# Half of the modulation loads moved from ahead of the first projection unit to beside units 0 and 1

## The chip, the cores and the metric

The kernel runs on one core of one Trainium2 chip. The metric is the device time of one execution in microseconds, lower is better. The parts of the core that matter here: TensorE (matrix products, PE in the profile, its weight loads PEld), VectorE (DVE), ScalarE (ACT), GpSimd (POOL), SyncE (SP), which issues all transfers from one queue, and the DMA engines.

## What is computed

A backbone of two layers on 512 latent tokens and 256 context tokens of width 1024. Only the beginning of layer 0 is touched:

```python
def rms_norm(x, g):
    xf = x.astype(jnp.float32)
    y = xf * lax.rsqrt(jnp.mean(xf * xf, axis=-1, keepdims=True) + EPS)
    return (y * g.astype(jnp.float32)).astype(x.dtype)

def modulate(x, g, shift, scale):
    return rms_norm(x, g) * (1 + scale) + shift
...
        mod_lat = jnp.split((silu_c @ w_mod[l] + b_mod[l])[:, None, :], N_MOD, axis=-1)
        mod_ctx = jnp.split((silu_cc @ w_mod[l] + b_mod[l])[None, None, :], N_MOD, axis=-1)
        a_lat = modulate(x, norm1_g[l], mod_lat[0], mod_lat[1])
        a_ctx = modulate(h, norm1_g[l], mod_ctx[0], mod_ctx[1])
...
    aq, ak, av, rq, rk, rv, rgf, rgb, fu = split_proj(a_lat @ w_in)
    cq, ck, cv, crq, crk, crv, crgf, crgb, cfu = split_proj(a_ctx @ w_in)
```

So the input projection needs the normalized tokens, and these need a shift (`mod[0]`) and a scale (`mod[1]`), each 1024 wide for two conditioning vectors, from 8 MB of `w_mod`.

## The kernel before

Everything is held transposed: X is [128, 8 tiles of features, 768 tokens]. Every fp32 operand of a large product is split into a high and a low part (`Whi`/`Wlo`, `Ahi`/`Alo`), and three products of the parts are added. ScalarE makes the high part of weights (`hi_static`), GpSimd the low one (`low_part`, `low_parts`: Wlo = raw - Whi); the semaphores are `hi_done` and `lo_done`.

The program is written by hand, one stream for each engine, and every stream runs in its written order. The input projection of layer 0 has 18 units. Units 0 to 3 make the first 512 columns: unit u multiplies the feature tiles 2u and 2u+1 into six banks (psA, psB, psS), 36 products of 512 columns. Unit 0 is `first_unit`, and unit 3, the last of its group, is `whole`: it goes bank by bank, and needs the low weights at its first product (`lo_done` 4).

**The modulation loads.** 16 loads of 512 KB (`modst`, six slots) bring the shift and scale rows of `w_mod`. Here they are m0 to m15, in the order of their issue. The even ones are for VectorE (`start(i)` takes m2i): each is multiplied with `csil` and added to an accumulator, four operations, so that after four loads a chunk of the scale (chunk 2, then chunk 3) is there as partial sums over partitions. The odd ones are for TensorE (`first_mod(i)` in TensorE's stream takes m(2i+1)): two products with a two-column stationary `csil` and 512 moving columns, four records in the trace, here called row products; four loads give a row of a shift chunk (chunk 0, then chunk 1). Chunk 0 and 2 serve the feature tiles 0 to 3, chunk 1 and 3 the tiles 4 to 7. A load into a slot waits for the one that used it last: m14 for `start(4)`, m15 for `first_mod(4)`.

VectorE's accumulator is summed over partitions by `mod_sums` (eight transposes on TensorE) and `mod_reduce` (two reductions and an addition on VectorE). TensorE's row is copied from PSUM by ScalarE (`row_copy`), turned by TensorE (`turn_row`) and gets its bias on VectorE (`shifts`).

**The norm.** X comes in as Xin (12 loads of 256 KB), is turned by TensorE (`x_turn(m)`, m = 0..7) and copied by ScalarE (`x_copy`); ScalarE squares it with sums. ScalarE's `norm_root` and VectorE's reciprocal give rstd, which `spread(0)` writes to ps6 (latent) and ps7 (context), one row on all partitions. Then for each tile j: VectorE `norm_full(0, j)` multiplies X by the gain and by ps6 or ps7 (two operations, `a_full`), ScalarE `norm_hi` adds the shift and rounds (`a_hi`; for odd j it writes a second, full copy too, and signals behind it), and the low part of A is VectorE's (`norm_low`, even j) or GpSimd's (`norm`, odd j, semaphore `a_lo_odd`).

In this program all 16 loads come first, and TensorE's stream has all row products, turns and sums ahead of `first_unit`, with filler products (`keep_clock_early`) between them. Behind the modulation loads SP issues the weights of units 0 and 1, then small loads (rope, sinks, tables), then the weights of unit 2.

Notation: `a_hi` n means that n tiles have signalled; "A 5" is the low part of A's tile 5; "W 2" is the low part of unit 2's weights.

## Time and profile before

| | us |
|---|---|
| time, median of 3 runs | 1581.91 (1579.78 to 1582.76) |
| the profiled execution | 1579.42 |
| its span on the core | 1577.5 |
| TensorE busy | 1551.3 (98%) |
| VectorE busy | 921.4 (58%) |
| ScalarE busy | 592.6 (38%) |
| GpSimd busy | 639.5 (41%) |

The span runs from the first to the last instruction of the core; 1.9 us of the execution lie around it. The page cuts the span into 40 slices of 39 us. TensorE is busy at nine tenths or more in all of them but the first, where it has six, so the start is the only stretch where it waits for long. DMA is at nine tenths in the first slice, and at two to four in most others. TensorE's granted clock is 0.999 of full speed over the span. "Busy" counts pipelined products whose times overlap; a step of work is therefore read as the distance between two starts.

### The profile page before, as it was taken

How to read it: one execution, taken by the hardware profiler on the slowest of the kernel's cores; microseconds unless marked ns; L12 is line 12 of the kernel's file. 1: busy time of each engine (PE TensorE's matmuls, PEld its weight loads, DVE VectorE, ACT ScalarE, POOL GpSimd, SP SyncE). 2: the span in 40 equal slices, each digit the busy share in tenths (PEclk: the TensorE clock that was granted, in tenths of full speed). 3: DMA queues.
4: the chain of work that ended last, by engine and by line, in shares of the span. 5: the costliest groups of instructions: out<-in, count | busy, mean ns of one | idle time of the engine just before them, and what ended most of it. 6: DMA issues, size and time to landing. Idle time of an engine off the chain costs nothing.

```text
span 1577.5 us, 22772 instructions
## 1 busy us (share of the span) xinstructions
PE 1551.3 (98%) x8718; PEld 1333.8 (85%) x8718; DVE 921.4 (58%) x1464; ACT 592.6 (38%) x982; POOL 639.5 (41%) x350
## 2 busy tenths in 40 slices
PE   6999999999999999999999999999999999999999
PEld 2888898989888888888888998888997888888887
DVE  5977988766765746545463668687645432233232
ACT  4632267743432121222212244435753422333332
POOL 0535478942333323233232464336004444444443
PEclk9999999999999999999999999999999999999999
DMA  9343203033243434344443433230102333333332
GB/s 329 126 142 105 68 18 108 27 108 107 74 131 120 134 107 134 108 133 133 115 126 107 145 111 106 68 92 29 41 4 83 89 94 95 101 97 93 94 105 95
DMA packets 169473, 161.73 MB, mean 103 GB/s; under 512 B 6548, under 2 KB 133928, under 8 KB 169384
## 3 DMA queue, kind: packets, MB, share of 16 engines
q1 hardware_dynamic: 169384, 160.48, 33.4%
q8 instruction: 63, 1.03, 0.3%
q14 instruction: 26, 0.21, 0.0%
HBM read 158.37 MB, written 2.10 MB: 102 GB/s over the span
## 4 chain that ended last, share of the span: by engine, by line
PE 92%; DVE 2%; DMA 1%; issue 1%; ACT 1%; POOL 1%; SPq 0%; POOLq 0%; ACTq 0%
PE psB L2195 31%; PE psA L2195 31%; PE psA L1930 6%; PE psB L1930 6%; PE ps L2165 4%; PE psS L1930 4%; PE psS L1743 2%; PE ps L1743 1%; DMA modst<-in_w_mod_dram 1%; PE psS L2086 1%; PE psA L2140 1%; PE psB L2140 1%; PE psS L1763 1%; PE psB L2141 1%; PE psA L2141 1%
## 5 line engine op out<-in xcount | busy, mean ns | idle before, releaser
L592 POOL TENSOR_TENSOR Wlo<-raw,Whi 128x1024 fp32r<-128x1024 f32 x156 | 380.7, 2441 | 729.5 <-ACT Whi L759 719.9
L759 ACT ACTIVATE Whi<-raw 128x1024 fp32r<-128x1024 f32 x181 | 191.7, 1059 | 677.2 <-PE psB L2195 346.4
L1347 DVE SCALAR_TENSOR_TENSOR X<-psB,modT,X 128x256 f32<-128x256 f32 (+1 forms) x104 | 67.2, 665 | 130.2 <-PE psB L2195 130.0
L1347 DVE SCALAR_TENSOR_TENSOR X<-psA,modT,X 128x256 f32<-128x256 f32 (+1 forms) x104 | 67.0, 663 | 89.6 <-PE psA L2195 89.6
L1177 DVE SCALAR_TENSOR_TENSOR macc<-modraw,csil,macc 128x512 f32<-128x512 f32 x126 | 111.8, 944 | 1.3 <-DMA modraw<-in_w_mod_dram 1.2
L1604 DVE TENSOR_TENSOR Hlo<-Ab,Hhi 128x512 fp32r<-128x512 f32 (+2 forms) x68 | 72.7, 1069 | 54.2 <-ACT Hhi L1050 54.2
L1602 DVE TENSOR_TENSOR Ab<-psA,Tb 128x512 f32<-128x512 f32 (+2 forms) x34 | 26.7, 784 | 129.4 <-ACT Tb L1042 129.4
L2195 PE MATMUL psB<-Ahi,Whi 128*128 128x512 f32 (+1 forms) x424 | 89.5, 357 | 0.0
L2195 PE MATMUL psB<-Ahi,Wlo 128*128 128x512 f32 (+1 forms) x424 | 88.9, 356 | 0.0
L2195 PE MATMUL psB<-Alo,Whi 128*128 128x512 f32 (+1 forms) x424 | 88.9, 356 | 0.0
L2195 PE MATMUL psA<-Ahi,Whi 128*128 128x512 f32 (+1 forms) x416 | 88.8, 358 | 0.0
L2195 PE MATMUL psA<-Alo,Whi 128*128 128x512 f32 (+1 forms) x416 | 87.8, 355 | 0.0
L2195 PE MATMUL psA<-Ahi,Wlo 128*128 128x512 f32 (+1 forms) x416 | 87.8, 355 | 0.0
L2195 PE MATMUL psA<-Hhi,Whi 128*128 128x512 f32 (+1 forms) x368 | 82.9, 358 | 0.0
L2195 PE MATMUL psB<-Hhi,Whi 128*128 128x512 f32 (+1 forms) x368 | 82.8, 358 | 0.1
L2195 PE MATMUL psB<-Hhi,Wlo 128*128 128x512 f32 (+1 forms) x368 | 82.2, 356 | 0.0
L2195 PE MATMUL psB<-Hlo,Whi 128*128 128x512 f32 (+1 forms) x368 | 82.1, 355 | 0.0
L2195 PE MATMUL psA<-Hlo,Whi 128*128 128x512 f32 (+1 forms) x368 | 82.1, 356 | 0.0
L2195 PE MATMUL psA<-Hhi,Wlo 128*128 128x512 f32 (+1 forms) x368 | 82.0, 355 | 0.0
L2165 PE MATMUL ps<-Pk,PTs 128*128 128x64 f32 x640 | 80.7, 270 | 1.2 <-DVE Alo L1536 0.9
L2195 PEld LDWEIGHTS psB<-Ahi,Wlo 128*128 128x128 f32 x424 | 71.6, 189 | 11.6
L2195 PEld LDWEIGHTS psB<-Alo,Whi 128*128 128x128 f32 x424 | 71.6, 189 | 11.6
(383 smaller groups left out, 3332.9 us busy)
## 6 DMA issues: line engine op xcount, KB each, us to landing
raw<-in_w_ff_dram SPq DMA_DIRECT2D x135, 512.0 KB, 4.0
modraw<-in_w_mod_dram SPq DMA_DIRECT2D x72, 512.0 KB, 4.2
raw<-in_w_in_dram SPq DMA_DIRECT2D x36, 512.0 KB, 3.7
modst<-in_w_mod_dram SPq DMA_DIRECT2D x16, 512.0 KB, 7.2
raw<-in_w_out_dram SPq DMA_DIRECT2D x16, 512.0 KB, 3.7
modat<-in_w_mod_dram SPq DMA_DIRECT2D x8, 512.0 KB, 4.6
macc<-in_w_ff_dram SPq DMA_DIRECT2D x5, 512.0 KB, 3.5
Xin<-in_x_dram SPq DMA_DIRECT2D x8, 256.0 KB, 7.9
```

What stands on the lines that cost most here:

```text
L592: nc.gpsimd.tensor_tensor(Wlo[:, s, :], raw[:, s, :], Whi[:, s, :], ALU.subtract).then_inc(S["lo_done"], 1)
L759: nc.scalar.activation(whis[slot], raws[slot], ACT.Copy).then_inc(S["hi_done"], 1)
L1177: ins = V.scalar_tensor_tensor(out=acc[:, s, :], in0=src[:, kk * MCH:(kk + 1) * MCH], scalar=col, in1=acc[:, s, :], op0=ALU.mult, op1=ALU.add)
L1347: last = V.scalar_tensor_tensor(out=X[:, m, c0:c1], in0=pair[p][:, c0:c1], scalar=modT[:, l, 8 * chunk + m, s:s + 1], in1=X[:, m, c0:c1], ...
L1602: V.tensor_tensor(Ab[:, k % 2, c0:c1], pair[k % 2][:, at + c0:at + c1], Tb[:, k % 2, c0:c1], ALU.mult).then_inc(S["h_full"], 1)
L1604: V.tensor_tensor(Hlo[:, hpar, k, c0:c1], Ab[:, k % 2, c0:c1], Hhi[:, hpar, k, c0:c1], ALU.subtract).then_inc(S["h_lo"], 1)
L1743: return nc.tensor.transpose(out, in_, ident[0:n, 0:n])
L1930: return mm(tokbank[t][:, 0:w], (Ahi, Alo)[x][:, k, t * P:(t + 1) * P], (Whi, Wlo)[y][:, uu % 2, cs], start=first, stop=fin)
L2140: mm(out, q, hi_keys, start=True, stop=False)
L2141: last = mm(out, q, lo_keys, start=False, stop=True)
L2165: last = mm((ps6, ps7)[b % 2][:, h * HD:(h + 1) * HD], PTs[:, it % 2, i * P:(i + 1) * P], Pk[:, kt, P + (h // 4) * HD:P + (h // 4 + 1) * H ...
L2195: last = mm(dst[:, c0:c1], weights[w][:, off:off + P], x[:, i, c0:c1], start=(opens and kind == 0 and i == 0), stop=(closes and kind == 2 ...
```

## The change

- Order of loads: x and ctx are issued behind m0 and m1, then m2 to m7, then the weights of units 0 and 1, then m8 to m15.
- TensorE: only the row products of m1, m3, m5, m7 stay ahead of `first_unit`. Those of m9 and m11 stand inside unit 0, those of m13 and m15 behind it. The turn of row 1 stands inside unit 1, and so do the sums of chunk 3, now eight products of the accumulator with a column of ones (`last_sums`) into ps7 in the place of eight transposes and two reductions. Twelve filler products stand ahead of unit 0.
- VectorE: norm_full 0 and 1 and norm_low 0 come first, then start(4) and start(5), norm_full 2 and 3, norm_low 2, start(6) and start(7), the two additions, the gain, and the tiles 4 to 7.
- ps7 is needed for the second row, so ScalarE copies its 256 columns of rstd for context tokens to `rb_context` in SBUF, and VectorE's context half of every norm_full(0, j) reads that.
- ScalarE: row_copy(1) stands behind the conversion of unit 2's weights, and that ahead of norm_hi 4. GpSimd: W 2 stands between A 3 and A 5, and W 3 behind A 7, one by one, where a loop did W 2 and W 3 behind A 7.

```diff
-    for i in range(16):
-            first_mod(i)
             if i == 2:
                 x_load(0, "xa_in")
-            if i == 4:
                 x_load(1, "xb_in")
-        for u in range(2):
-            w_load(u, u, r2(u), proj_src(0, u), True)
+            if i == 8:
+                for u in range(2):
+                    w_load(u, u, r2(u), proj_src(0, u), True)
+            first_mod(i)
...
-                norm(0)
-                low_parts(2, 10)
+                norm(0, 1, 4)
+                low_part(2)
+                norm(0, 5)
+                low_part(3)
+                low_parts(4, 10)
...
+        act.wait_ge(S["rb_ready"], 1)
+        nc.scalar.activation(rb_context, ps7[:, 0:CTX], ACT.Copy).then_inc(S["rb_copied"], 1)
         hi_static(0)
...
-                    if k == 1:
-                        hi_static(1)
+                    if k in (1, 3):
+                        hi_static(1 + k // 2)
+                    if k == 3:
+                        row_copy(1)
...
-        for i in range(6):
+        for i in range(4):
             start(i)
         mod_reduce(0, 2, 0)
-        shifts(0)
-        start(6)
-        norm_root(0)
-        start(7)
+        first_chunk(0, "row_turned", 1, psS[:, 0:8])
         dve.wait_ge(S["mod_evac"], 2)
         gain(0, 0, 0, 4)
+        norm_root(0)
         dve.wait_ge(S["x_ready"], KT)
         norm_full(0, 0)
-        shifts(1)
         norm_full(0, 1)
-        mod_reduce(0, 3, 1, 2, (psS[:, 0:512], psS[:, 512:1024]))
+        start(4)
+        start(5)
+        norm_full(0, 2)
+        norm_full(0, 3)
+        for i in range(6, 8):
+            start(i)
+        first_chunk(1, "row_turned", 2, ps7[:, 0:8])
+        first_chunk(3, "modp_ready", 2, ps7[:, 8:16])
         dve.wait_ge(S["mod_evac"], 4)
         gain(0, 0, 4, 8)
-        for j in range(2, KT):
+        for j in range(4, KT):
             norm_full(0, j)
...
+        def last_sums():
+
+            pe.wait_ge(S["mod_first"], 8)
+            pe.wait_ge(S["mod_step"], 24)
+            pe.wait_ge(S["mod_evac"], 3)
+            for t in range(4):
+                for s in range(2):
+                    at = 8 + 2 * t + s
+                    last = mm(ps7[:, at:at + 1], macc[:, s, t * P:(t + 1) * P], ones[:, :], start=(t == 0 and s == 0), stop=(t == 3 and s == 1))
+            last.then_inc(S["modp_ready"], 1)
...
                 pe.wait_ge(S["lo_done"], 1)
                 for t in ts:
                     products(0, 0, 1, t)
+                pe.wait_ge(S["rb_copied"], 1)
+                first_mod(4)
                 pe.wait_ge(S["a_hi"], 2)
                 for t in ts:
                     products(1, 0, 0, t)
                     products(1, 0, 1, t)
+                first_mod(5)
                 pe.wait_ge(*a_lo(0, 1))
...
                     first_unit()
+                    first_mod(6)
+                    first_mod(7)
                     continue
...
+                if l == 0 and u == 1:
+                    turn_row(1)
...
+                    if l == 0 and u == 1:
+                        last_sums()
```

VectorE, from the first norm_full of layer 0, before (the names are output <- inputs; Tb and Ab hold the tiles of `norm_full`, ps7 the context half of rstd):

```order
L1239 SCALAR_TENSOR_TENSOR Tb<-X,gs,ps7 128x256 [waits rb_ready,x_ready,dve]
L1239 SCALAR_TENSOR_TENSOR Tb<-X,gs,ps6 128x512
L1319 TENSOR_TENSOR modT<-psS,bmodT 128x8 [waits row_turned]
L1239 SCALAR_TENSOR_TENSOR Tb<-X,gs,ps7 128x256
L1239 SCALAR_TENSOR_TENSOR Tb<-X,gs,ps6 128x512
L1227 SCALAR_TENSOR_TENSOR Alo<-Tb,modT,Ahi 128x256 [waits a_hi]
L1227 SCALAR_TENSOR_TENSOR Alo<-Tb,modT,Ahi 128x512
L1204 TENSOR_REDUCE modT<-psS 128x4 [waits modp_ready]
L1204 TENSOR_REDUCE modT<-psS 128x4
L1207 TENSOR_TENSOR modT<-modT,bmodT 128x8 [waits mod_red]
L1213 SCALAR_TENSOR_TENSOR gs<-modT,parT 128x8 [waits mod_evac]
```

and the same place after (sqb is where `rb_context` lies):

```order
L1247 SCALAR_TENSOR_TENSOR Tb<-X,gs,sqb 128x256
L1247 SCALAR_TENSOR_TENSOR Tb<-X,gs,ps6 128x512
L1233 SCALAR_TENSOR_TENSOR Alo<-Tb,modT,Ahi 128x256 [waits a_hi]
L1233 SCALAR_TENSOR_TENSOR Alo<-Tb,modT,Ahi 128x512
L1181 TENSOR_SCALAR macc<-modst,csil 128x512 [waits modst_in2]
L1181 TENSOR_SCALAR macc<-modst,csil 128x512
L1183 SCALAR_TENSOR_TENSOR macc<-modst,csil,macc 128x512 [waits mod_step] x2
L1183 SCALAR_TENSOR_TENSOR macc<-modst,csil,macc 128x512 [waits mod_step,modst_in4]
L1183 SCALAR_TENSOR_TENSOR macc<-modst,csil,macc 128x512 [waits mod_first]
L1183 SCALAR_TENSOR_TENSOR macc<-modst,csil,macc 128x512 [waits mod_step] x2
L1247 SCALAR_TENSOR_TENSOR Ab<-X,gs,sqb 128x256
```

start(4) and start(5), eight operations on macc, now stand between the tiles 1 and 2, where the reductions stood; start(6) and start(7) follow behind tile 3.

TensorE in unit 1 before, behind its first high products:

```order
L1930 MATMUL psS<-Whi,Ahi 128x512 x4
L1930 MATMUL psA<-Whi,Alo 128x512 [waits a_lo_even]
L1930 MATMUL psA<-Whi,Alo 128x512
L1930 MATMUL psB<-Whi,Alo 128x512 x2
L1930 MATMUL psS<-Whi,Alo 128x512 x2
L1930 MATMUL psA<-Whi,Alo 128x512 [waits a_lo_odd]
L1930 MATMUL psA<-Whi,Alo 128x512
L1930 MATMUL psB<-Whi,Alo 128x512 x2
L1930 MATMUL psS<-Whi,Alo 128x512 x2
L1930 MATMUL psA<-Wlo,Ahi 128x512 [waits lo_done]
```

and after:

```order
L1956 MATMUL psS<-Whi,Ahi 128x512 x4
L1755 MATMUL ps<-ident,sqb 128x2 [waits row_copied]
L1755 MATMUL ps<-ident,sqb 128x2 x3
L1956 MATMUL psA<-Whi,Alo 128x512 [waits a_lo_even]
...
L1956 MATMUL psS<-Whi,Alo 128x512 x2
L1868 MATMUL ps<-ones,macc 128x1 [waits mod_evac,mod_step,mod_first]
L1868 MATMUL ps<-ones,macc 128x1 x7
L1956 MATMUL psA<-Wlo,Ahi 128x512 [waits lo_done]
```

The turn of row 1 and the sums of chunk 3 now stand inside the unit, each with a wait of its own: for ScalarE's copy, and for VectorE's start(7) and chunk 1's addition.

## Rows read from the trace of the kernel before

**Rows 1.** The page: span, and busy time of TensorE (share) xinstructions.

```profile
span 1577.5 us, 22772 instructions
...
PE 1551.3 (98%) x8718; PEld 1333.8 (85%) x8718; DVE 921.4 (58%) x1464; ACT 592.6 (38%) x982; POOL 639.5 (41%) x350
```

**Rows 2.** Windows: stretch, length, busy PE, PEld, DVE, ACT, POOL, PEclk, DMA, GB/s.

```profile
20.00:25.00 5.00, 3.29 (x17) 1.55 (x16) 0.95 (x2) 4.05 (x11) 0.00 (x0) 1.00 1.05 388
```

**Rows 3.** Timeline of TensorE: start, duration, engine, line, operation, out<-in, shape xcount [idle].

```profile
15.21 1.52 PE L1743 MATMUL psA<-ident,Xin 128*128 128x128 f32 x6 [2.90 <-DMA Xin<-in_ctx_dram]
...
26.61 1.88 PE L1837 MATMUL psS<-modst,csil 128*2 128x512 f32 x4
...
30.21 1.09 PE L1743 MATMUL ps<-ident,macc 128*128 128x128 f32 x8
31.24 5.31 PE L1837 MATMUL psS<-modst,csil 128*2 128x512 f32 x12
37.20 0.84 PE L1743 MATMUL ps<-ident,rstd 128*128 128x128 f32 x6 [0.66 <-DVE rstd L1220]
...
40.87 0.40 PE L1743 MATMUL psS<-ident,sqb 2*128 2x2 f32 x4
...
44.33 0.47 PE L1891 MATMUL psA<-Whi,Ahi 128*128 128x512 f32 x1
...
52.75 1.22 PE L1930 MATMUL psA<-Whi,Ahi 128*128 128x512 f32 x4
...
69.44 0.39 PE L1930 MATMUL psA<-Whi,Ahi 128*128 128x512 f32 x1
```

**Rows 4.** Timeline of VectorE.

```profile
24.69 2.74 DVE L1177 SCALAR_TENSOR_TENSOR macc<-modst,csil,macc 128x512 f32<-128x512 f32 x4 [4.04 <-DMA modst<-in_w_mod_dram]
...
32.75 1.28 DVE L1204 TENSOR_REDUCE modT<-ps 128x4 f32<-128x512 f32 x2
...
39.79 1.14 DVE L1239 SCALAR_TENSOR_TENSOR Tb<-X,gs,ps 128x256 f32<-128x256 f32 x2
...
42.47 1.15 DVE L1227 SCALAR_TENSOR_TENSOR Alo<-Tb,modT,Ahi 128x256 fp32r<-128x256 f32 x2
...
48.60 2.19 DVE L1239 SCALAR_TENSOR_TENSOR Ab<-X,gs,ps 128x256 f32<-128x256 f32 x4
...
104.18 1.29 DVE L1204 TENSOR_REDUCE modT<-ps 128x4 f32<-128x512 f32 x2 [7.37 <-PE ps L1743]
```

**Rows 5.** Timeline of ScalarE.

```profile
39.89 0.59 ACT L865 ACTIVATE sqb<-psS 2x512 f32<-2x512 f32 x1 [5.33 <-PE psS L1837]
...
44.60 1.04 ACT L759 ACTIVATE Whi<-raw 128x1024 fp32r<-128x1024 f32 x1
49.77 2.17 ACT L809 ACTIVATE Ahi<-Ab,modT 128x256 fp32r<-128x256 f32 x4 [4.12 <-DVE Ab L1239]
51.84 1.11 ACT L809 ACTIVATE Ab<-Ab,modT 128x256 f32<-128x256 f32 x2
```

**Rows 6.** Timeline of GpSimd and VectorE, where both work, single instructions.

```profile
43.79 2.40 POOL L592 TENSOR_TENSOR Wlo<-raw,Whi 128x1024 fp32r<-128x1024 f32 x1 [9.63 <-DVE Alo L1227]
...
48.50 1.85 POOL L620 TENSOR_TENSOR Alo<-Tb,Ahi 128x768 fp32r<-128x768 f32 x1
...
60.36 2.08 DVE L1175 TENSOR_SCALAR macc<-modraw,csil 128x512 f32<-128x512 f32 x1
...
62.36 2.89 DVE L1177 SCALAR_TENSOR_TENSOR macc<-modraw,csil,macc 128x512 f32<-128x512 f32 x1
64.66 2.84 POOL L592 TENSOR_TENSOR Wlo<-raw,Whi 128x1024 fp32r<-128x1024 f32 x1
```

**Rows 7.** Timeline of TensorE: four products of a tile with a column of ones.

```profile
376.48 0.95 PE L1763 MATMUL psS<-ones,Ab 128*128 128x1 f32 x8
```

**Rows 8.** SP's issues of the small loads (timeline), and landing times of modst (tile).

```profile
34.58 0.47 SPq L472 DMA_DIRECT2D rope<-in_table_dram  x1
...
37.95 0.91 SPq L437 DMA_DIRECT2D tmpt<-in_fourier_w_dram  x2
...
DMA to landing us min/median/max: 3.8/7.2/11.5
```

More of the change, by code:

```diff
@@ L613, in rotate, with norm @@
             nc.gpsimd.tensor_tensor(v, tmp[:, 0:256], tmp[:, 256:512], ALU.add).then_inc(out_sem, 1)
-        def norm(n):
+        def norm(n, j0=1, j1=KT):
             c0, c1 = NORMS[n][2]
-            for j in range(1, KT, 2):
+            for j in range(j0, j1, 2):
                 pool.wait_ge(S["a_hi"], 8 * n + j + 1)
@@ L878, in _ @@
         x_square(1, 1)
+        for t in range(2, NT):
+            x_square(t, 1)
         row_copy(0)
+        norm_root(0)
         x_copy(6)
-        x_square(2, 1)
         x_copy(7)
-        for t in (3, 4, 5):
-            x_square(t, 1)
-        norm_root(0)
-        row_copy(1)
+        act.wait_ge(S["rb_ready"], 1)
+        nc.scalar.activation(rb_context, ps7[:, 0:CTX], ACT.Copy).then_inc(S["rb_copied"], 1)
         hi_static(0)
@@ L1836, in first_mod @@
             for kk in range(2):
-                last = mm(psS[0:2, 512 * c:512 * c + 512], csil[:, 2 * part + kk, :], modst[:, slot, kk * MCH:(kk + 1) * MCH],
+                last = mm((psS, ps7)[c][0:2, 0:512], csil[:, 2 * part + kk, :], modst[:, slot, kk * MCH:(kk + 1) * MCH],
                           start=(part == 0 and kk == 0), stop=(part == 3 and kk == 1))
```

59 lines of the change are left out of this document (30 added, 29 removed).

## Prediction

> **What bounds the kernel now.** I read the page first: TensorE is busy for 1551.3 of 1577.5 us [rows 1], so a change counts only by what it does to TensorE's wait or work. Then TensorE's timeline of the start [rows 3]: the first product of unit 0 starts at 44.33, unit 1 at 52.75, unit 3 at 69.44, without a gap from there on. What stands ahead of 44.33 is waiting, filler and preparation. There DMA is full, 388 GB/s [rows 2], 1.35 us for a load of 0.52 MB. With m0 to m15 for the 16 modulation loads (even ones for VectorE, odd ones for TensorE): VectorE starts on m6 when it lands at 24.69 [rows 4]. Last I read VectorE, ScalarE and GpSimd behind 44 us [rows 4 to 6], since half the preparation now moves there.
>
> **The start of unit 0.** Ahead of m6 lie the same bytes as before (m0 to m5 and all of x and ctx), so it lands at 24.7 again, and m7 at 26.1. m2 to m5 are now behind x: m2 at 19.3, m3 at 20.7. Two chains lead to the sums of chunk 2. VectorE: 19.3 plus three units of 2.74 [rows 4] = 27.5. TensorE: x is there 1.35 sooner than 15.21 [rows 3] and the first four turns are done by about 19.5, then it waits for m3; from 20.7 three pairs of row products of 1.77 (twelve records in 5.31) and four turns of some 0.72 end at 28.9. TensorE's is later. Then the sums 1.05 (29.9) [rows 3], reduction, two additions, gain and reciprocal 2.0 (31.95) [rows 4], spread 0.84 and 0.2 of handing over (33.0) [rows 3], the new copy of ps7 into rb_context, 256 columns, about 0.5 by the 0.59 of 512 columns on two rows [rows 5] (33.5), two norm_full 2.2, norm_low 1.15 [rows 4]: unit 0 starts at **37.2** instead of 44.33, a gain of 7.1. Much of that chain lay under loads before. The filler (12 products) ends near 35.6 and isn't in the way. Bounds: VectorE can't end m6 before 27.5, which would give 35.7; products of the first turns that stay at 1.2 GHz longer (1.52 a group, [rows 3]) could give 39. I take 37.2.
>
> **What TensorE does more behind the start.** Row products of m9, m11, m13, m15: 4 x 1.77 = 7.1; the second row's turn 0.35 (0.40 in [rows 3]); eight products with `ones`, twice the four of [rows 7], at most 1.9, I take 1.6. All lie in TensorE's stream, between products that nothing delayed: **9.0**. So with no wait at all the change would lose 1.9. Bounds 8.7 to 9.4.
>
> **The new waits.** Now VectorE's second half runs beside GpSimd's low parts. The trace has that case at 60 to 68 us [rows 6]: a multiplication of modraw with csil took 2.08, and a multiply-add 2.89, where four of m6 took 2.74 together [rows 4]; it ended 0.5 after GpSimd's instruction; GpSimd's next one in turn was 2.84 instead of 2.40. They take turns. What is held up reads and writes SBUF alone; operations that read PSUM aren't: norm_full, 2.19 for four parts, ran beside GpSimd's 1.85 at 48.50 [rows 4, 6].
>
> VectorE after 37.1, by turns: start(4) has four such operations and three instructions of GpSimd stand beside it (low parts of W 0 and 1, 2.40 each; of A 1, 1.85), which all wait for the same moment: 2.3 + 6.3 = 8.6, to 45.7. start(5) alone, 2.74: 48.4. norm_full 2 and 3, 2.2: 50.6. norm_low 2: 51.8. start(6) beside A 3 and W 2: 2.74 + 1.8: 56.2 (GpSimd can do A 3 only after ScalarE's copy at 52.8). start(7) beside the rest of W 2: 2.74 + 2.3: **61.2**. m14 isn't late for it: its slot comes free with start(4), 45.7, and it lands 3.8 later (the least in [rows 8]), near 49.6; m15 near 50.9.
>
> TensorE meanwhile, with 0.23 a product (36 in 8.42, [rows 3]): unit 0's first 18 products to 41.5, row products to 43.3, 12 products 46.1, row products 47.9, 6 products 49.2, row products 51.0, the last with m15 to 52.7; unit 1's first 12 to 55.6. Then the turn of row 1 needs ScalarE's row_copy(1), which stands behind hi_static(2), which needs the weights of unit 2. SP issues these after m14, m15 and the small loads, which took it from 34.58 to 38.86 [rows 8]: so near 51, landed 54.9, conversion 1.04 [rows 5], row copy 0.59: 56.6. **Wait one, 1.1.** The turn and 12 products end at 59.8. The sums need start(7) and chunk 1's addition, 61.4. **Wait two, 1.6.** Sums to 63.0, 12 products to 65.75.
>
> Behind the sums: addition and gain 0.5, norm_full 4 and 5, ScalarE's high parts. In the trace a_hi of an odd tile comes 4.35 after its pair's norm_full starts (48.60 to 52.95, [rows 4, 5]). So a_hi 6 at 63.5 + 4.4 = 68.0; unit 2's second product needs it. **Wait three, 2.0.** Unit 2 has 35 products left, to 76.0. Unit 3 needs all of lo_done 4, and the chain to it is: norm_full 6 and 7, of which 7 is held back by GpSimd's A 5 (68.0 to 69.8), as its context part now reads rb_context in SBUF: 71.0; ScalarE's pair 2.2 (73.25); GpSimd's A 7, 1.85, and W 3, 2.4, the last put behind norm here: 77.6 to 78.2. **Wait four, 1.9.** Unit 3 starts at 77.9 against 69.44.
>
> The sum is -7.1 + 9.0 + 1.1 + 1.6 + 2.0 + 1.9 = **+8.5 us**. None is given back: unit 3 and all after it hang on TensorE alone, and VectorE, then 4.5 us behind where it was against TensorE, has 7.37 idle ahead of 104.18 [rows 4] to make it good. Unit 0's wait for the low part of W 0 is nought, by 0.1 only (ready 40.1, needed 40.2).
>
> A rule to weigh: the Trainium skill, SBUF — State Buffer, section "SBUF: two separate sides", says VectorE with two SBUF inputs and GpSimd lock each other out for a whole instruction. The rows at 60 to 68 us agree (2.89 against some 0.7). It also speaks against moving ps7's half to rb_context; a norm_full beside GpSimd that reads only PSUM and X was not held back. By that rule the copy costs the 1.8 at norm_full 7, already in wait four by the rows: the sum is +8.5 with it and +6.7 without.
>
> **Against the runs.** The profiled execution took 1579.4 (its span 1577.5 and 1.9 around it); 8.5 more is 1587.9. The median shown is 2.5 above it, which gives 1590.4. I say 1590.0, as such offsets are the runs' spread.
>
> **The rivals.**
> (A) The forecast, +6 to +10.5, chance 0.60.
> (B) VectorE and GpSimd get past each other: at the two pairs of start() the operations of VectorE slip in between, start(7) ends near 51. Then waits one and two go (2.7), the lock at norm_full 7 too (1.8): +4.0, 1586. For it: GpSimd idles much of 37 to 60, and A 3 may fall elsewhere. Against: the rows of that form that met an instruction of GpSimd at 60 to 68 us [rows 6] all show the turns. 0.17.
> (C) Not slower. The place is the chain from m6 to unit 0, the price 1.05 + 0.5: if the sums go at 27.5 and every copy is hidden, unit 0 starts at 35.7 and saves 8.6, and if VectorE keeps ahead so that no wait is left, 9.0 - 8.6 = +0.4, 1582. It decides from the point at which unit 0 starts sooner than 35.3 and waits are nil. For it: the start is limited by m6 only in the bound. Against: what is added to TensorE is more than the best start gives back, and waits two to four come from chains counted from that same start. 0.13, of which 0.04 for faster.
> (D) TensorE's clock falls. At 15 us the turns ran at 1.2 GHz, after a wait of 2.9 (1.52 for six, [rows 3]); the change has idle stretches of 1.5 to 2 us around 20, 31, 36 us and at the four waits. If one of them drops it as unit 0 starts, some 15 products take twice 0.23: 3.4 more, +12, 1594. 0.10.
>
> **Numbers.** The likeliest is A, 1590.0. The range 1585 to 1594.5 holds A, D's middle and most of B, and leaves out C and the edges, under 0.2. A measurement of this kernel tells 0.2% (3.2 us) from no change: A and D are all slower, of B five sixths, of C a part at its upper end: slower 0.85, same 0.11, faster 0.04.
>
> **What would show it.** In the timeline of after: unit 0's first product at 37.2 (35.7 to 39); in unit 0 and behind it row products of 1.77 each; a gap ahead of the eight `ones` products, with VectorE's macc as releaser; a gap of 2 in unit 2 behind its first product, released by ScalarE; one ahead of unit 3, released by GpSimd's W 3; unit 3 at 77.9; VectorE operations of start(4) of over 2 us. Wrong would be the sum if start(7) ended by 55 (then B), or if unit 0 started before 35.

## The result, and the profile after

The changed kernel takes **1597.2 us** (median of 4 runs, 1594.92 to 1598.85) against 1581.83 (4 runs of before beside it): ratio 1.0102, 95% interval 1.0089 to 1.0114. The forecast was 1590.0 with a range to 1594.5: the sign was right, the time lies above the range. Measured a second time, with other runs of before beside it, the changed kernel gave 1593.7 (ratio 1.0076, 1.0060 to 1.0091), which is inside the range, near its upper end; both measurements count, and the clock goes with more than half of the difference (last section). The profiled execution took 1594.92, its span is 1593.0: 15.5 more than before's 1577.5, where the forecast was 8.5.

TensorE is busy for 1560.4 us, 98% of the span as before (answers to [rows 1]).

TensorE's timeline (start, duration, engine, line, operation, out<-in, shape, count, [idle before <- releaser]); these rows answer to [rows 3]:

```profile
20.52 3.47 PE L1849 MATMUL psS<-modst,csil 128*2 128x512 f32 x4 [2.17 <-DMA modst<-in_w_mod_dram]
...
33.78 1.01 PE L1755 MATMUL ps<-ident,rstd 128*128 128x128 f32 x6 [1.84 <-DVE rstd L1226]
34.58 4.35 PE L1836 MATMUL psA<-ident 128*128 128x128 f32 x24
...
38.98 0.47 PE L1912 MATMUL psA<-Whi,Ahi 128*128 128x512 f32 x1
...
51.42 3.59 PE L1849 MATMUL ps<-modst,csil 128*2 128x512 f32 x8
...
61.04 0.40 PE L1755 MATMUL ps<-ident,sqb 2*128 2x2 f32 x4 [3.08 <-ACT sqb L868]
61.37 1.03 PE L1956 MATMUL psA<-Whi,Alo 128*128 128x512 f32 x2
...
65.34 0.63 PE L1956 MATMUL psS<-Whi,Alo 128*128 128x512 f32 x2
65.81 1.84 PE L1868 MATMUL ps<-ones,macc 128*128 128x1 f32 x16
...
72.51 0.97 PE L1956 MATMUL psA<-Whi,Ahi 128*128 128x512 f32 x3 [1.50 <-ACT Tb L812]
...
82.52 0.50 PE L1956 MATMUL psA<-Whi,Ahi 128*128 128x512 f32 x1 [1.78 <-POOL Wlo L596]
```

Read down: unit 0 starts at 38.98 (before 44.33, forecast 37.2). The row products are where they were expected and cost what was expected. At 61.04 stands wait one, 3.08 long. At 61.37 two products take 1.03, at 65.34 two of the same kind take 0.63: the clock. No wait stands ahead of the sums at 65.81 (wait two is missing). Waits three and four are there, 1.50 and 1.78, with the forecast releasers. Unit 3 starts at 82.52, 13.1 later than before.

Windows of the changed kernel (stretch, length, busy PE, PEld, DVE, ACT, POOL, granted PE clock, DMA share, GB/s):

```profile
60.00:65.00 5.00, 3.96 (x13) 3.17 (x14) 0.17 (x1) 0.98 (x2) 2.36 (x1) 0.66 0.60 182
...
255.00:260.00 5.00, 3.77 (x26) 3.02 (x23) 4.97 (x11) 3.13 (x10) 3.67 (x2) 0.96 0.38 109
260.00:265.00 5.00, 5.00 (x30) 4.57 (x29) 3.18 (x8) 3.78 (x8) 1.03 (x1) 0.70 1.03 348
```

The same place of the program in before, 13 to 14 us earlier:

```profile
246.00:251.00 5.00, 5.00 (x42) 4.68 (x41) 4.50 (x10) 4.86 (x11) 0.00 (x0) 1.00 0.87 278
```

A mean of 0.66 over 5 us in the changed kernel means that part of the stretch ran at the lower level, 1.2 GHz: 0.34 x 5 = **1.7 us** lost where TensorE is never idle. The rows agree: from the turn to the sums it takes 4.77 here and 3.23 in e1 below, where the clock stays up, so 1.5 is seen of the 1.7. The same sum, 1.5 + 0.2, holds for the fall at 260, where before has 1.00. All falls of the changed kernel: around 21, 35, 62 and 260 us.

ScalarE, and SP's issue of unit 2's weights (timeline), ahead of wait one:

```profile
59.45 1.06 ACT L762 ACTIVATE Whi<-raw 128x1024 fp32r<-128x1024 f32 x1 [5.71 <-DMA raw<-in_w_in_dram]
60.41 0.57 ACT L868 ACTIVATE sqb<-ps 2x512 f32<-2x512 f32 x1
...
52.18 1.77 SPq L401 DMA_DIRECT2D raw<-in_w_in_dram  x2
```

VectorE and GpSimd in the changed kernel (answers to [rows 4, 6]):

```profile
38.75 3.03 DVE L1181 TENSOR_SCALAR macc<-modst,csil 128x512 f32<-128x512 f32 x2
41.70 7.76 DVE L1183 SCALAR_TENSOR_TENSOR macc<-modst,csil,macc 128x512 f32<-128x512 f32 x6
...
52.77 6.95 DVE L1183 SCALAR_TENSOR_TENSOR macc<-modst,csil,macc 128x512 f32<-128x512 f32 x8
...
72.55 2.11 DVE L1247 SCALAR_TENSOR_TENSOR Ab<-X,gs,sqb 128x256 f32<-128x256 f32 x1
...
39.00 5.02 POOL L592 TENSOR_TENSOR Wlo<-raw,Whi 128x1024 fp32r<-128x1024 f32 x2 [7.89 <-DVE Alo L1233]
43.98 2.28 POOL L620 TENSOR_TENSOR Alo<-Tb,Ahi 128x768 fp32r<-128x768 f32 x1
...
72.54 1.85 POOL L620 TENSOR_TENSOR Alo<-Tb,Ahi 128x768 fp32r<-128x768 f32 x1 [9.59 <-ACT Tb L812]
```

start(4) and start(5) take 10.7 us (38.75 to 49.4) beside GpSimd's three instructions, where they took 5.1 in e6 below. SP issues m14 at 46.84, when start(4) has given its slot free, and only behind that m15, the small loads and the weights of unit 2; the DMA engines move nothing from 40 to 45 us (share 0.00). The context part of norm_full 7 takes 2.11 beside GpSimd's A 5, where the same form takes 0.48 elsewhere.

### The profile page after: what moved, and what is told of

Read it like the earlier page. It is cut to its first block, busy times and chain, and to the rows that moved or that the text cites. A ratio compares the mean times of both kernels' runs of the same rounds, so it can differ in the third digit from the quotient of the medians.

```text
span 1593.0 us, 22775 instructions
## 1 busy us (share of the span) xinstructions
PE 1560.4 (98%) x8722; PEld 1338.5 (84%) x8722; DVE 927.5 (58%) x1462; ACT 593.0 (37%) x983; POOL 641.8 (40%) x350
## 3 DMA queue, kind: packets, MB, share of 16 engines
q8 instruction: 63, 1.03, 0.3%
## 4 chain that ended last, share of the span: by engine, by line
PE 89%; DVE 4%; ACT 2%; issue 2%; DMA 1%; SPq 1%; POOL 1%; POOLq 0%; ACTq 0%; DVEq 0%
PE psA L2225 30%; PE psB L2225 30%; PE psA L1956 5%; PE psB L1956 5%; PE ps L2195 4%; PE psS L1956 4%; PE psS L1755 2%; PE ps L1755 2%; PE psS L2116 1%; PE psA L2170 1%; PE psB L2170 1%; DMA modst<-in_w_mod_dram 1%; PE psB L2171 1%; PE psS L1775 1%; PE psA L2171 1%
## 5 line engine op out<-in xcount | busy, mean ns | idle before, releaser
L592 POOL TENSOR_TENSOR Wlo<-raw,Whi 128x1024 fp32r<-128x1024 f32 x154 | 376.6, 2446 | 724.1 <-ACT Whi L762 716.2
```

Of the source, the lines that this page charges most:

```text
L592: nc.gpsimd.tensor_tensor(Wlo[:, s, :], raw[:, s, :], Whi[:, s, :], ALU.subtract).then_inc(S["lo_done"], 1)
```

## The experiments

My theory from the changed kernel's trace: the overrun is the late landing of unit 2's weights, which holds the small row copy and with it TensorE, and falls of TensorE's clock behind that and other waits. The rivals: the row products themselves on TensorE, VectorE held up by GpSimd, and the chain to W 3. Ten kernels leave nothing out; three leave out work, as their texts say; two are copies. Times of before beside them had medians of 1579.9 to 1581.6.

| kernel | unit 0 | sums | unit 3 | unit 3 - unit 0 | span | median us (runs) | ratio, 95% |
|---|---|---|---|---|---|---|---|
| before | 44.33 | | 69.44 | 25.1 | 1577.5 | 1581.83 (4) | 1 |
| before again | 44.08 | | 69.17 | 25.1 | 1577.2 | 1579.08 (1) | |
| changed | 38.98 | 65.81 | 82.52 | 43.5 | 1593.0 | 1597.2 (4) | 1.0089-1.0114 |
| changed again | 39.01 | 65.89 | 82.59 | 43.6 | 1593.1 | 1593.7 (4) | 1.0060-1.0091 |
| e1 row first | 39.89 | 61.99 | 78.69 | 38.8 | 1589.4 | 1590.68 (5) | 1.0046-1.0074 |
| e2 weights first | 37.48 | 60.56 | 77.35 | 39.9 | 1588.4 | 1589.07 (4) | 1.0036-1.0077 |
| e3 filler | 37.03 | 63.77 | 80.92 | 43.9 | 1594.4 | 1594.0 (4) | 1.0064-1.0095 |
| e4 W 3 early | 39.09 | 61.19 | 77.97 | 38.9 | 1588.5 | 1587.64 (6) | 1.0022-1.0046 |
| e5 short rows | 37.42 | 59.75 | 76.47 | 39.1 | 1586.6 | 1589.11 (4) | 1.0037-1.0079 |
| e6 short GpSimd | 38.93 | 61.00 | 77.72 | 38.8 | 1586.0 | 1590.13 (5) | 1.0035-1.0068 |
| e7 both | 37.35 | 52.96 | 71.55 | 34.2 | 1580.3 | 1584.08 (10) | 1.0008-1.0028 |
| e8 unit 2's order | 39.00 | 61.07 | 77.75 | 38.8 | 1587.4 | 1589.33 (5) | 1.0030-1.0063 |
| a3 22 zero products | 38.86 | 65.89 | 82.59 | 43.7 | 1592.5 | 1594.97 (4) | 1.0074-1.0104 |
| a4 12 zero products | 38.79 | 63.70 | 80.41 | 41.6 | 1590.4 | 1593.92 (4) | 1.0069-1.0100 |
| v1 together | 37.10 | 58.12 | 74.09 | 37.0 | 1584.4 | 1584.4 (11) | 1.0012-1.0030 |
| v2 filled | 37.34 | 59.71 | 72.72 | 35.4 | 1583.7 | 1585.18 (10) | 1.0020-1.0039 |
| v3 filled less | 37.17 | 58.18 | 72.55 | 35.4 | 1580.7 | 1584.18 (11) | 1.0011-1.0029 |

### Wait one: the row copy behind the weights

**e1: the row copy first.** ScalarE's small copy of row 1 stands ahead of the conversion of unit 2's weights.

```diff
-                    if k in (1, 3):
-                        hi_static(1 + k // 2)
                     if k == 3:
                         row_copy(1)
+                    if k in (1, 3):
+                        hi_static(1 + k // 2)
```

> The changed kernel, with one thing exchanged in ScalarE's order: the copy of row 1 now stands ahead of the conversion of unit 2's weights. Theory (the turn of row 1 waited 3.1 us only because the copy stood behind weights that landed at 59.45): the copy runs at about 55.6, TensorE turns the row at 57.9 without a wait and keeps 2.4 GHz through unit 1, the sums with ones start at about 61.0 instead of 65.8, unit 3 at 77.7 instead of 82.5, and the time falls by 4.9 us, to about 1592. Rival (VectorE's start(7), which ended at 59.7, and the chains behind it are the bound anyway): less than 1.5 us, 1596.

TensorE's timeline of e1:

```profile
20.38 3.57 PE L1849 MATMUL psS<-modst,csil 128*2 128x512 f32 x4 [3.35 <-DMA modst<-in_w_mod_dram]
...
39.89 0.47 PE L1912 MATMUL psA<-Whi,Ahi 128*128 128x512 f32 x1 [1.50 <-DVE Alo L1233]
...
61.99 1.84 PE L1868 MATMUL ps<-ones,macc 128*128 128x1 f32 x16
...
78.69 0.50 PE L1956 MATMUL psA<-Whi,Ahi 128*128 128x512 f32 x1 [1.76 <-POOL Wlo L596]
```

The wait at the turn is gone, no wait took its place at the sums, and the clock stays at 1.00 from 60 to 65. From unit 0 to unit 3 it takes 38.8 instead of 43.5: 4.7 = 3.1 of wait + 1.7 of clock. The median is 6.5 below the changed kernel's first measurement and 3.0 below its second. In this one profile unit 0 is 0.9 later, because the clock stayed low for longer behind the wait for m3: not only its row products (3.57 for four records, 1.88 at full clock) but also the turns behind them (the mean is 0.50 from 20 to 25 us, 0.66 in the changed kernel).

**e2: the weights first.** The weights of units 2 and 3 are issued ahead of the small loads.

```diff
+        for u in (2, 3):
+            w_load(u, u % 2, r2(u % 2), proj_src(0, u), False)
         late_ = S["late_in"]
...
-                if u0 + u >= 2:
+                if u0 + u >= 4:
```

> The changed kernel, with the loads of the weights of units 2 and 3 issued ahead of the eight small loads (rope, sinks, tables) and ScalarE's order as it was. Theory (the landing of unit 2's weights sets the turn of row 1): they land near 53 instead of 59.45, the wait at the turn goes as in the run with the copy first, and the time falls by 4 to 5 us, to about 1592.5. Rival (the turn waits for the last row product and the copy, not for the weights): no change, 1597.

```profile
60.56 1.92 PE L1870 MATMUL ps<-ones,macc 128*128 128x1 f32 x16 [0.83 <-DVE modT L1329]
...
67.34 0.96 PE L1958 MATMUL psA<-Whi,Ahi 128*128 128x512 f32 x3 [0.18 <-ACT Tb L814]
```

The other way to the same end: the weights come early enough, the turn waits for nothing, and now the sums wait 0.83 for VectorE. So wait one is the landing of the weights, and behind it VectorE is late next, by under 1 us, not by 1.6. Part of that lateness is e2's own: GpSimd makes W 2 sooner and so beside start(6) and start(7), which take 9.08 for the 6.95 of the changed kernel. Behind the sums the clock falls here (0.81 and 0.85 from 60 to 70 us, 1.7 together), and wait three is down to 0.18. The median agrees with e1.

### The clock ahead of unit 0

**e3: filler in the two gaps.** Eight short products in each of two idle stretches ahead of unit 0.

```diff
+        for i in range(8):
+            mm(psS[:, 512:640], ident[:, :], ident[:, :], start=True, stop=True)
         first_mod(1)
...
         turn_row(0)
+        for i in range(8):
+            mm(psS[:, 512:640], ident[:, :], ident[:, :], start=True, stop=True)
         pe.wait_ge(S["mod_evac"], 1)
         spread(0)
```

> The changed kernel, with eight filler products of TensorE ahead of the row products of m3 and eight ahead of the spread of rstd, where it waited 2.2 and 1.8 us. Theory (the two stretches at 1.2 GHz from 20.7 and 34.3 us are what made unit 0 start at 38.98 instead of the 37.2 forecast): both go, the row products of m3 take 1.9 instead of 3.5, unit 0 starts at 37.8, and the time falls by about 1, to 1596. Rival (ScalarE's squares, which ended at 30.9, set the start): unit 0 at 38.8, no change.

```profile
20.39 1.88 PE L1849 MATMUL psS<-modst,csil 128*2 128x512 f32 x4 [1.58 <-DMA modst<-in_w_mod_dram]
...
37.03 0.47 PE L1916 MATMUL psA<-Whi,Ahi 128*128 128x512 f32 x1 [1.51 <-DVE Alo L1233]
```

Without the falls around 21 and 35 us unit 0 starts at 37.03: the forecast's 37.2 is the kernel's start at full clock, and the 1.8 by which it was missed is clock. Nearly all of it is the first fall: e2 and e7 have only the second, and start at 37.48 and 37.35; e5, which has neither, starts at 37.42. But the median is 1594.0, no better than the changed kernel measured again: in this profile the clock fell at 62, 82 and 260 us, once more than in the changed kernel behind unit 0.

### Wait four and wait three

**e4: unit 3's weights early.** e1, and ScalarE converts unit 3's weights ahead of norm_hi 7, GpSimd makes W 3 ahead of A 7.

```diff
-                norm(0, 5)
+                norm(0, 5, 7)
                 low_part(3)
+                norm(0, 7)
...
                 for k in range(KT):
+                    if k == 7:
+                        hi_static(3)
                     norm_hi(0, k)
...
-                if l or u:
+                if l or u > 1:
                     hi_static(u0 + u + 2)
```

> The run with the row's copy first, and beside it the weights of unit 3 earlier: ScalarE converts them ahead of its last norm_hi, GpSimd makes their low part ahead of the low part of A 7. Theory (unit 3 waited 1.8 us for GpSimd's W 3, which stood behind A 7): that wait goes, unit 3 follows unit 2 directly, and the time is 1.8 below the run with the copy first, 1590.5. Rival (A 7, now last, takes the place of W 3 and unit 3 stops at its fourth group of products instead): the same as the run with the copy first, 1592.

Windows and GpSimd's timeline of e4:

```profile
65.00:70.00 5.00, 3.07 (x10) 1.98 (x9) 4.86 (x8) 4.71 (x9) 1.65 (x1) 0.84 0.35 106
70.00:75.00 5.00, 5.00 (x19) 4.05 (x19) 5.00 (x5) 3.97 (x6) 4.21 (x3) 0.82 0.00 0
```

```profile
70.62 2.39 POOL L596 TENSOR_TENSOR Wlo<-raw,Whi 128x1024 fp32r<-128x1024 f32 x1 [0.44 <-ACT Whi L763]
```

W 3 is ready at 73.0 and unit 3 starts without a wait at 77.97. In the profile nothing is gained (38.9 from unit 0, as in e1), since a clock fall behind wait three took the 1.7 back (0.84 and 0.82 are 0.8 + 0.9). Over six runs the median is 3.0 below e1, more than the wait. Its executions differ as the clock does: spans of 1588.5 at a mean clock of 0.996, 1582.6 at 0.999 and 1582.1 at 1.000.

**e8: unit 2 tile by tile.** e1, and unit 2 does all three products of tile 4 ahead of tile 5's first.

```diff
+                if l == 0 and u == 2:
+                    pe.wait_ge(S["hi_done"], 3)
+                    for kk in range(2):
+                        pe.wait_ge(S["a_hi"], 5 + kk)
+                        for x, y in ((0, 0), (0, 1), (1, 0)):
...
+                            for t in range(NT):
+                                last = mm(tokbank[t][:, 0:512], (Ahi, Alo)[x][:, 4 + kk, t * P:(t + 1) * P],
+                                          (Whi, Wlo)[y][:, 0, kk * 512:(kk + 1) * 512], start=False, stop=False)
```

> This is e1_row_first with unit 2's matrix products ordered as unit 0's are: all three products of feature tile 4 before the first of tile 5. Nothing is left out. In e1_row_first TensorE waits 1.50 for ScalarE's high part of feature tile 5 after three products of the first kind. Theory: 'wait three is only the order': the wait goes, unit 3 at about 77 (from 78.69), the whole 1.5 us below e1_row_first: 1589.2. Rival 'unit 3 waits for the low part of its weights in any case' (1.76 in e1_row_first, GpSimd): the wait at unit 2 goes and that at unit 3 grows by the same, no change: 1590.7.

The wait list of e8 between 60 and 90 us (waited for: total, times, longest):

```profile
PE psA L1970 <- POOL Wlo L596: 3.5, 1, 3.5
```

The rival holds: wait three is gone, and wait four is 3.50 instead of 1.76. From unit 0 to unit 3 it takes 38.8 as in e1. Without wait three the chain from the sums to GpSimd's W 3 still sets unit 3; that e8's median is 1.35 below e1's isn't explained by this, and the intervals of the two overlap.

### What holds the sums: rows, locks, or both

e5, e6 and e7 stand on e1. e5 cuts the row products of m9, m11, m13 and m15 to 16 of 512 columns, e6 cuts GpSimd's low parts of W 0, W 1, A 1 and A 3 to 64 columns, e7 does both.

```diff
-                last = mm((psS, ps7)[c][0:2, 0:512], csil[:, 2 * part + kk, :], modst[:, slot, kk * MCH:(kk + 1) * MCH],
+                w_ = 16 if c else 512
+                last = mm((psS, ps7)[c][0:2, 0:w_], csil[:, 2 * part + kk, :], modst[:, slot, kk * MCH:kk * MCH + w_],
```

```diff
-                    nc.gpsimd.tensor_tensor(Wlo[:, s, :], raw[:, s, :], Whi[:, s, :], ALU.subtract).then_inc(S["lo_done"], 1)
+                    w_ = 64 if u1 == 2 else UE
+                    nc.gpsimd.tensor_tensor(Wlo[:, s, 0:w_], raw[:, s, 0:w_], Whi[:, s, 0:w_], ALU.subtract).then_inc(S["lo_done"], 1)
...
+                if n == 0 and j < 4:
+                    c1 = c0 + 64
```

> This is e1_row_first with the products of the second half of each modulation row (row products of m9, m11, m13, m15) cut to 16 of their 512 columns: part of the modulation is left out, nothing else. TensorE's stretch between unit 0 and the sums loses four row halves. Theory 'VectorE's chain sets the start of the sums': TensorE comes to the sums about 4 x 1.77 / 2 = 3.5 us to 7 us earlier but start(7) on VectorE still ends near 59.9, so the sums start no earlier than 60.5, against 61.99 in e1_row_first; unit 3 at about 77.5 against 78.69, and the whole is 1 to 1.5 us below e1_row_first: 1589.4. Rival 'the row products lie on the path': the sums start near 55 to 58, unit 3 near 72 to 74, the whole 3.5 to 7 us below e1_row_first: 1584 to 1587.

> This is e1_row_first with GpSimd's low parts of the weights of units 0 and 1 and of feature tiles 1 and 3 cut to 64 columns each (the rest is zero): part of the projection's low halves is left out. GpSimd then holds the shared SBUF port for much less of the time in which VectorE does start(4) to start(7). Theory 'VectorE waits for GpSimd at the port, but TensorE arrives at the sums at 61 anyway': the eight products of a start (52.8 to 59.7, 0.87 each) fall to near 0.75 each and start(7) ends near 53 to 55; TensorE's sums stay at 61 to 62, unit 3 near 78, the whole 0 to 1 us below e1_row_first: 1590. Rival 'the port is the whole delay': sums near 56, unit 3 near 73, the whole 5 us below e1_row_first: 1586.

> Both cuts, of e5_short_rows and of e6_short_pool. If the two chains (TensorE's rows, VectorE's starts) end within 1.5 us of each other at the sums, only both cuts together bring the sums forward: sums at 53 to 56, unit 3 at 70 to 72, the whole 6 to 7.5 us below e1_row_first: 1583 to 1585, while e5 and e6 alone give 0 to 1.5 us each. Rival 'one of them alone binds': e7 is no better than the better of e5 and e6. Third: the sums come sooner, but unit 2 then waits for its feature tiles (norm_hi 5 to 7 of ScalarE and the low parts of GpSimd) or for its weights (landed 59.5), and less than 4 us of it is kept.

SP (m14 and m15) and TensorE in e5, SP (m14, then m15) and VectorE in e6, TensorE in e7 (timelines):

```profile
45.29 0.88 SPq L455 DMA_DIRECT2D modst<-in_w_mod_dram  x2
...
50.41 0.27 PE L1850 MATMUL ps<-modst,csil 128*2 128x16 f32 x4 [3.55 <-DMA modst<-in_w_mod_dram]
```

```profile
41.00 0.37 SPq L455 DMA_DIRECT2D modst<-in_w_mod_dram  x1
...
45.09 0.37 SPq L455 DMA_DIRECT2D modst<-in_w_mod_dram  x1
...
38.70 0.94 DVE L1188 TENSOR_SCALAR macc<-modst,csil 128x512 f32<-128x512 f32 x2
39.57 4.19 DVE L1190 SCALAR_TENSOR_TENSOR macc<-modst,csil,macc 128x512 f32<-128x512 f32 x6
```

```profile
52.96 1.84 PE L1876 MATMUL ps<-ones,macc 128*128 128x1 f32 x16
...
59.54 0.47 PE L1964 MATMUL psA<-Whi,Ahi 128*128 128x512 f32 x1 [1.85 <-ACT Ahi L819]
...
61.52 0.96 PE L1964 MATMUL psA<-Whi,Ahi 128*128 128x512 f32 x3 [1.50 <-ACT Tb L819]
```

From unit 0 to the sums: e1 22.1, e5 22.3, e6 22.1, e7 **15.6**. Neither cut alone brings the sums nearer to unit 0; both together bring them 6.5 forward. Two chains of nearly the same length lead there. One is TensorE's own work with the row products. The other is VectorE, slowed by GpSimd (start(4) and start(5) take 5.1 in e6, 10.7 in the changed kernel), and it reaches TensorE in a way that I hadn't thought of: e5's 3.55 wait isn't for the accumulator, it is for m15. TensorE had read m9 out of m15's slot at 42, but SP issues in its written order, and m15 stands behind m14, whose slot start(4) gives free: SP issues m14 at 45.29 and m15 0.4 later. In e6, where start(4) is over sooner, m14 goes at 41.00, and m15 at 45.09, behind TensorE's products with m9. Behind the 3.55 the clock of e5 falls (0.88, 0.50 and 0.93 in the windows from 45 to 60 us), and a wait of 0.84 for ScalarE lies in it. VectorE's start(7) and addition end at 58.25, so without the fall the sums of e5 could have come 1.5 sooner, not more: 20.8 from unit 0. "Neither alone" is exact for e6, and for e5 it holds within that 1.5. The median of e7 is 6.6 below e1, of e5 1.6 and of e6 0.6, as unit 3 is 7.1, 2.2 and 1.0 sooner. And e7, with both costs all but gone, is still 0.08 to 0.28% slower than before: then unit 2's waits for its feature tiles (1.85 and 1.50) lie bare, and the clock falls behind them (0.78 and 0.88 from 60 to 70 us).

### The clock falls

**The two copies.**

> The changed kernel once more, unchanged. If the stretches in which TensorE's granted clock is 0.50 are fixed by the program, the profile shows the same ones as before (21 to 24, 34 to 38, 61 to 65 and 259 to 263 us) and unit 3 starts at 82.5 again. If it is a matter of the single execution, one or two of them are missing or elsewhere, unit 3 and the span move by 1.5 to 2 us for each, and the median stays at 1597.

> The kernel before once more, unchanged. If it never has the stretch at clock 0.50 near 246 us that the changed one has at 260, the granted clock is 1.00 from 20 us on, with the single low stretch at 15 to 19 us; if that is chance, a second profile shows a low stretch where the first had none, and its span is 1.5 to 2 us longer than 1577.5.

Windows of the changed kernel's second profile:

```profile
60.00:65.00 5.00, 3.84 (x13) 3.11 (x14) 0.17 (x1) 1.11 (x2) 2.36 (x1) 0.66 0.63 190
260.00:265.00 5.00, 5.00 (x32) 4.61 (x31) 2.96 (x7) 3.78 (x8) 0.49 (x1) 0.73 0.97 300
```

The falls stand at the same places, unit 3 starts at 82.59. Before's second profile has none behind 20 us, and not even the one at 15 to 19 us of the first (unit 0 starts at 44.08 for 44.33 and the span is 1577.2, so that one cost at most 0.3). The expectation for the copy of the changed kernel held for the places and not for the median, which is 3.5 lower.

**a3 and a4: no idle stretch ahead of the fall at 62 us.** The changed kernel with products of zeros, added to psA, ahead of the turn.

```diff
                 if l == 0 and u == 1:
+                    pe.wait_ge(S["sd_zero"], 1)
+                    for i in range(22):
+                        mm(psA[:, 0:P], SD[:, 0, 0, 0, :], ident[:, :], start=False, stop=False)
                     turn_row(1)
```

> The changed kernel with 22 short TensorE products of zeros (128x128, about 0.11 us each, added to psA, which changes nothing in it) ahead of the turn of row 1 in unit 1, where TensorE waits 3.1 us for ScalarE; nothing is left out. Theory 'the idle stretch there is what the clock falls behind': the granted clock stays 1.00 from 60 to 65 us, turn and 12 products take 3.1 instead of 4.8, the sums start at 64.1 instead of 65.8, unit 3 at 80.9 instead of 82.5, the whole 1.7 us below the changed kernel: 1592 to 1595.5 (it gave 1597.2 and 1593.7). Rival 'the fall is not tied to that idle stretch' (as the one near 260 us, which has only idle stretches of 0.86 and 0.37 before it, both also in the trace of the kernel before, where no fall follows): the fall comes all the same, at the same place or a few us on, and nothing is gained.

> The changed kernel with 12 products of zeros ahead of the turn of row 1 in unit 1 instead of the 22 of a3_fill_turn, since one took 0.23 us there (two records each, 44 records in 5.07) and 22 outlasted the wait; 12 take 2.8 of the 3.1. Nothing is left out. Theory 'the fall at 61 us goes with the idle stretch ahead of it and costs 1.7': granted clock 1.00 from 57 to 66, the sums at 64.2, unit 3 at 80.9 (82.5 in the changed kernel), the whole 1.5 to 1.7 us below it: 1592 to 1595.5. Rival: unit 3 waits for GpSimd's split in any case and the gain in front of it is lost: 82.5.

TensorE's timeline of a3, then timeline and windows of a4:

```profile
57.65 5.07 PE L1986 MATMUL psA<-ident,SD 128*128 128x128 f32 x44
62.66 0.41 PE L1755 MATMUL ps<-ident,sqb 2*128 2x2 f32 x4
...
65.89 1.84 PE L1868 MATMUL ps<-ones,macc 128*128 128x1 f32 x16
```

```profile
57.58 2.84 PE L1986 MATMUL psA<-ident,SD 128*128 128x128 f32 x24
60.51 0.41 PE L1755 MATMUL ps<-ident,sqb 2*128 2x2 f32 x4
...
63.70 1.84 PE L1868 MATMUL ps<-ones,macc 128*128 128x1 f32 x16
```

```profile
60.00:65.00 5.00, 4.91 (x33) 4.21 (x32) 0.17 (x1) 0.46 (x1) 2.38 (x1) 1.00 0.60 186
80.00:85.00 5.00, 4.59 (x14) 3.66 (x15) 4.79 (x8) 1.23 (x3) 3.10 (x2) 0.69 0.58 182
```

I had sized a zero product at 0.11; it takes 0.23, being two records, so a3's filler outlasted the wait by 1.6 and cost what the clock gave. Still, in both the clock stays at 1.00 there, and from the turn to the sums it takes 3.2 instead of 4.8. In a4 this moves unit 3 to 80.41, 2.1 sooner. But then the clock falls at 80 to 85 us, behind wait four, where it had not before, and the medians (1594.97, 1593.92) can't be told from 1593.7. Filling one wait removes the fall behind it and doesn't bring the time down.

### A combined version

**v1** has e1, e4, e8 and filler ahead of unit 0, and a second accumulator for chunk 3. SP issues the weights of units 0 and 1 behind m9. In it m9's and m11's row products stand in the gap ahead of unit 0, and start(4) ahead of the reduction. **v2** and **v3** add zero products ahead of the sums and inside unit 0 (14 and 5, or 7 and 2). Nothing is left out.

```diff
-        keep_clock_early(12)
+        keep_clock_early(2)
+        pe.wait_ge(S["rb_copied"], 1)
+        first_mod(4)
+        first_mod(5)
...
-        for i in range(4):
+        for i in range(5):
             start(i)
```

> A version made of what the runs so far point to; nothing of the computation is left out. Against the changed kernel: the small row copy ahead of the conversion of unit 2's weights (e1_row_first); eight and four short TensorE products in the two gaps ahead of the spread (so that the clock has no idle stretch there); the row products of m8 to m11 moved from unit 0 to the gap ahead of unit 0; VectorE's start(4) moved ahead of the reduction of chunk 2, with a second accumulator; unit 3's weights converted and split ahead of feature tile 7 (e4_w3_early); unit 2's products tile by tile (e8_unit2_order). Theory 'the four waits and the two lock spans are all there is': unit 0 at 37.1, unit 1 at 49, the sums near 55 to 57, unit 3 at 67.6 (69.44 before the change), the whole at 1579 to 1580, that is 0.1 to 0.2% below before. Rival 'what the row products and the sums cost TensorE stays, and the clock falls once or twice on the way (1.7 to 1.9 us each)': 1581 to 1585.

> v1_together with 14 such products of zeros ahead of the sums of unit 1 and 5 ahead of the wait for GpSimd's low part of feature tile 1; nothing is left out. Theory: no clock fall at 58 to 66 us, sums still at 58.1 (VectorE's start(7) sets them), unit 3 at 72.3 instead of 74.1, the whole at 1582 to 1583 against 1584.4 of v1_together, that is within 0.1% of before. Rival: the fall moves to another place: 1584.

> v2_filled with 7 and 2 products of zeros instead of 14 and 5, for the same reason: there they pushed the sums from 58.1 to 59.7. Nothing is left out. Theory: sums at 58.1, no fall of the clock at 56 to 66, unit 3 at 71.1 (72.7 in v2_filled, 74.1 in v1_together, 69.44 before the change), the whole at 1581.5 to 1583, within 0.2% of before (1579.9 to 1581.8 in these runs). Rival: the fall comes back in part: 1584.

TensorE in v1, a window of v3:

```profile
58.12 2.42 PE L1871 MATMUL ps<-ones,ropeg 128*128 128x1 f32 x16 [1.66 <-DVE modT L1331]
```

```profile
60.00:65.00 5.00, 5.00 (x16) 4.01 (x17) 4.67 (x11) 3.19 (x6) 0.02 (x1) 0.66 0.00 0
```

v1 and v3 end 0.2% above before, v2 0.3%: the best of this design, and not better than before. The forecasts for them were missed by 4 to 5 us (v1), 2 to 3 (v2) and 1 to 3 (v3); the rivals beside them, 1581 to 1585 for v1 and 1584 for the others, came within 1.2 us. VectorE comes to the sums at 58, not at 55 to 57. In v1 the clock falls behind that wait (0.93, 0.50 and 0.88 from 55 to 70 us): from the sums to unit 3 it takes 16.0, and 13.0 in v2, where it stays up. It falls behind the sums in v3 too, although no idle stretch over 0.3 us lies ahead of it there. v3's profile closes the account: unit 3 3.1 later than before, the span 3.2 longer.

## Why the prediction was right and where it was wrong

The sign was right and the size wrong, and two steps of the sum failed. The larger: the sum has no term for TensorE's clock, which stands only in rival D, and the clock's falls cost about 5 of the 7.0 us by which the profiled execution overran. The smaller: wait one, 1.1 in the sum, was 3.08, because the weights of unit 2 landed 7.3 us after their issue and not 3.9.

The account of the profiled execution, in us against before:

| term | forecast | measured | from |
|---|---|---|---|
| unit 0 sooner | -7.1 | -5.35 | 44.33 to 38.98 |
| rows, turn, sums on TensorE | +9.0 | +9.2 | 7.15 + 0.33 + 1.71 |
| wait one | +1.1 | +3.08 | the turn |
| clock fall at 62 | 0 | +1.7 | windows |
| wait two | +1.6 | 0 | no idle ahead of the sums |
| wait three | +2.0 | +1.5 | tile 5 |
| wait four | +1.9 | +1.8 | W 3 |
| small pieces in units 0 to 3 | 0 | +1.2 | what is left to 13.1 |
| behind unit 3 | 0 | +2.4 | 1510.5 against 1508.1 |
| sum | +8.5 | +15.5 | |

- **The start of unit 0.** The chain was right: at full clock it starts at 37.03 (e3) and 37.10 (v1), for 37.2. What failed was the choice among the bounds. The text named 39 for turns that stay at 1.2 GHz, and took 37.2. The clock fell behind the waits for m3 (2.17) and for rstd (1.84); the filler, said to end near 35.6, ended at 38.9 and was itself at half clock.
- **TensorE's added work** was right to 0.2. From it alone follows the sign: 9.2 added to the engine that bounds the kernel, 7.3 gained even at full clock (44.33 to 37.03).
- **Wait one** had the right place and releaser and the wrong size. The step that failed is "SP issues these ... near 51, landed 54.9". The issue began at 52.18, 1.2 late, and the weights landed at 59.45: 7.3 later, not 3.9. TensorE itself came to the turn 2.4 later than forecast, so 2.0 more of wait is left. I took the least of the three landing times in [rows 8] (3.8, 7.2, 11.5) for a load that stands behind ten others on one queue; the median was the nearer row (5.9 to 7.6 in the changed kernel, e1 and e3 to e8). e1 and e2 show from two sides that this wait was the obstacle there. Not tried: the weights of unit 2 ahead of m14, which SP waits for while the DMA engines are idle.
- **Wait two** did not come: the larger wait one hid it. start(7) ended at 59.7, for 61.2, since W 2, forecast beside it, was made only from 60.58, behind the late weights. With wait one gone it is 0.83 (e2) and nothing (e1). That there are two chains of nearly equal length (e7) was in the numbers, 59.8 and 61.4, but I hadn't said that taking away one gives nothing.
- **Waits three and four** were right to 0.5, and the lock too: the row copied to SBUF, 2.11 for 0.48, is 1.6 of the 1.8 named at norm_full 7, and start(4) and start(5) took 10.7 for the 11.3 forecast. The Trainium skill, SBUF — State Buffer, section "SBUF: two separate sides", says that an operation of VectorE with two inputs in SBUF and one of GpSimd that reads SBUF shut each other out; here the rows and e6 agree (5.1 and 10.7 us for the same two units of work). The two waits don't simply add, though: when e8 took wait three away, wait four grew by as much.
- **Rival D, the clock,** was the mechanism of the overrun beside A, with a chance of 0.10 and a single fall priced. In the profile there are the two ahead of unit 0, one of 1.7 at 62, and one of 1.7 at 260, where I expected nothing. Against the forecast that is 1.75 (unit 0's late start) + 1.7 + 1.7 = 5.15 of 7.0. The 1.75 is shown by e3 and the fall at 62 by e1, a3 and a4; that at 260 is read from the windows, and no run was made against it. The rest is wait one (+2.0), waits two to four (-2.2 together), and 2.1 in small pieces.
- "None is given back": right. VectorE waits 2.26 ahead of the reductions at 117.39, where it waited 7.37 ahead of them at 104.18 before: its slack took the delay up, and TensorE got nothing back.
- B and C are refuted: the locks are there (e6), and unit 0 started neither before 35.3 nor without waits behind it.

## What to carry to other kernels

When work moves from ahead of a bound engine to inside its stream, compare the added time on that engine with the gain at the start first; here 9.2 against 7.3 at full clock decided the sign, and ten variants could only bring the loss from 1.0% down to 0.2%. For a load behind others in a queue take the median landing time, not the least, and look at what stands behind the instruction that waits for it: a 0.6 us copy behind a conversion that waited for the load cost 3.1 in wait and 1.5 to 1.7 in clock. And where a change cuts a dense stream by new waits, price the clock behind every one of them: both profiles of the changed kernel have four falls, two of them behind unit 0's start, and that belongs into the sum, not into a rival with a chance of 0.10.
